# Modulation of a hybrid DeltaNet / RG-LRU layer in four parts of two channel tiles, with the loads, the parameter rows, two clearings and a weight split moved around it

## The chip, the cores and the metric

One core of one Trainium2 chip runs the whole program. The time is that of the device from the first to the last instruction, in microseconds (us); runs are given by their median. Engines are called TensorE (PE in the rows), VectorE (DVE), ScalarE (ACT), GpSimd (POOL) and SyncE (SP); nearly all loads of this stage are issued by SyncE.

## The reference

One layer of a diffusion trunk, for 128 context tokens and 1024 latent tokens of 1024 channels. What matters here is its head:

```python
shift, scale, gate = jnp.split(mod, 3, axis=-1)      # mod = silu(c) @ w_mod + b_mod, for c and for c_ctx
h = rmsnorm(x, p['norm_w']) * (1 + scale) + shift
proj = h @ p['w_in']                                 # 1024 x 6176, all in float32
```

Then come a gated DeltaNet of 8 heads, an RG-LRU, two output projections merged by gates, one more projection, a residual and a last RMSNorm. `w_mod` is 1024 x 3072; shift and scale are its first 2048 columns.

## The kernel before

All work is on tiles of 128 channels or 128 tokens: KT = 8 channel tiles `k`, NT = 9 token tiles `t` (one of context, eight latent), and NG = 3 groups `g` of three token tiles. Float32 products are made exact enough by splitting both sides in a high and a low float32r part: three matmuls for each tile. Each engine has its own hand-written list of instructions (`front_sync`, `front_gpsimd`, and the ScalarE, TensorE and VectorE functions of `front_stage`), and counters (`S["..."]`) order them. The lists are strictly sequential, so an instruction that waits holds all behind it on its engine.

The opening of the kernel, up to the first projection, goes so:

- **x.** A token tile of 512 KB is loaded (`x_load`), ScalarE squares and sums it (L736), GpSimd makes the reciprocal root (L518, L520), ScalarE scales the tile (`normalise`, L730), TensorE turns it in eight transposes (`turn_x`, L1019) and VectorE copies it from PSUM to `xt` in two halves (L1435).
- **Modulation.** `mod_load(n)` brings 512 KB of `w_mod`: one channel tile's rows, half of the shift and half of the scale columns, in runs of 2 KB. `modulate(n)` (L1010) multiplies it by silu(c) for both conditions, four matmuls of 256 columns in four column groups of the array; a float32 matmul stands in the trace as two records. Loads 0 to 7 make half 0 (gain and shift of channel tiles 0 to 3), loads 8 to 15 half 1 (tiles 4 to 7). `gain_and_shift` then copies a half to SBUF (L1450), has it turned (`turn_columns`, L1026) and adds the parameters (L1456 to L1459).
- **Parameters.** 18 small loads (`small_rows_in`, L397) are turned by three transposes (L1079) and copied to `par` (L1438) and scaled (L1440 to L1442). `wglo`, the low part of the gate weights, is made at L1445.
- **Rows.** For each channel tile VectorE writes gain times x plus shift into one of two buffers `hf` (L1464 context, L1468 latent), ScalarE rounds it to `hhi` (L748; by groups at L753 for tiles 0 and 4; L758 makes the latent rows of tiles 1 and 5), and VectorE subtracts for `hlo` (L1479, `low_rows`). TensorE runs `first_high(k)` (L1033, L1034, gate columns at L1037) and `first_low(k)` (L1043, L1048) of the first weight block; the second block starts with `project(1, 0)` (L134 to L136).
- **Filling.** `idle(n)` is n matmuls of the identity (L142) into a bank that nobody reads.
- **GpSimd** clears `w1` and `w2` (L553, L554) as soon as `modulate` has read the first four weight loads, which lie in them; then `low(0)` and `low(1)` (L528) make the low parts of weight blocks 0 and 1 from what ScalarE's `high(0)`, `high(1)` (L621) rounded.

In TensorE's list the modulations of half 0 stand between the turns of x, those of half 1 between channel tiles 0 to 3: three, three and two.

Of the kernel before, what the change touches and what calls it, by code (L numbers as in the profile page):

```python
# [125 lines left out]
def v3(ap):  # L126
    return ap.rearrange("p (j c) -> p j c", c=P)
# [35 lines left out]
def front_stage(nc, R, A, oa, rows, decay_rows, gate_rows, W):  # L163


    with ExitStack() as ctx:
# [24 lines left out]
        with nc.sbuf_tensor("wg_hl", [P, KT, 8 * H], F32R) as wghl:  # L191
# [25 lines left out]
        modrow = row2[:, 200:712].rearrange("p (a c) -> p a c", a=2)  # L217
# [48 lines left out]
            "wm2", "wm3", "x0", "x1", "x2", "x3", "wg_in", "h_fa", "rows_t", "par_done", "mod_k", "mod_row", "mod_t", "mod", "x_sq", "x_ms", "x_rstd", "x_n", "x_t",  # L266
# [75 lines left out]
        def mod_bank(half_):  # L342
            return bank[(2, 0)[half_]]

        def rows_done(k, g=NG - 1):
            return k + (NG - 1) * ((k + 3) // 4) + (g + 1 if k % 4 == 0 else 1)
# [10 lines left out]
        def front_sync(sp):  # L357
# [27 lines left out]
            def mod_load(n):  # L385
                half_, k = divmod(n, KT)
                if n >= NW:
                    sp.wait_ge(S[f"wm{n % NW}"], 16 * (n // NW))
                if n >= NOWN:
                    sp.wait_ge(S["mod_k"], KT)  # L390
                src = A["w_mod"][0, k * P:(k + 1) * P, 0:2 * D].rearrange("p (a c) -> p a c", a=2)
                sp.dma_start(wmod[n].rearrange("p (a c) -> p a c", a=2), src[:, :, half_ * 512:(half_ + 1) * 512]
                             ).then_inc(S[f"wm{n % NW}"], 16)
# [7 lines left out]
            x_load(0)  # L401
            x_load(1)
            mod_load(0)
            x_load(2)
            x_load(3)
            mod_load(1)
# [4 lines left out]
            mod_load(2)  # L411
            small_rows_in(1)
            x_load(6)
            x_load(7)
            mod_load(3)
            x_load(8)
            load(0)
            mod_load(4)
            sp.dma_start(wg, A["w_in"][0, :, 6 * D:6 * D + 4 * H].rearrange("(k p) n -> p k n", p=P)
                         ).then_inc(S["wg_in"], 16)  # L420
            for n in range(5, 2 * KT):
                mod_load(n)
# [87 lines left out]
        def front_gpsimd(pool):  # L510
# [11 lines left out]
            for padded in row:  # L522
                pool.memset(padded[:, 0:PAD_L], 0.0)
                pool.memset(padded[:, PAD_L + CTX:PAD_L + CTX + GAP], 0.0)
                pool.memset(padded[:, RAW - 1:RAW], 0.0).then_inc(S["clear"], 1)
# [25 lines left out]

            pool.wait_ge(S["mod_k"], 4)
# [63 lines left out]
        def front_scalar(act):  # L616
# [115 lines left out]
            for t in range(NT):  # L732
# [4 lines left out]
                if t:  # L737
                    normalise(t - 1)
# [6 lines left out]
            def high_rows(k):  # L745
                if k % 4:
# [221 lines left out]
        def front_tensor(pe):  # L968
# [29 lines left out]
            for half_ in range(2):  # L998
                for j in range(2):
                    keep_busy(pe, bank[half_][:, j * P:(j + 1) * P], ident, 4)  # L1000
# [5 lines left out]
            def modulate(n):  # L1006
                half_, k = divmod(n, KT)
                pe.wait_ge(S[f"wm{n % NW}"], 16 * (n // NW + 1))
                for i in range(Q):
                    mm = pe.matmul(bank[half_][mod_rows(i), 0:256], sc[:, :, k], wmod[n][:, i * 256:(i + 1) * 256],  # L1010
                                   start=(k == 0), stop=(k == KT - 1))
                mm.then_inc(S["mod_k"], 1)

            def turn_x(n):
                if n >= 2:
                    pe.wait_ge(S["x_e"], n - 1)
                pe.wait_ge(S["x_n"], n + 1)
# [5 lines left out]
            def turn_columns(half_):  # L1023
                pe.wait_ge(S["mod_row"], half_ + 1)
                for j in range(2):
                    mm = pe.transpose(mod_bank(half_)[:, j * P:(j + 1) * P], modrow[:, half_, j * P:(j + 1) * P], ident)  # L1026
                mm.then_inc(S["mod_t"], 1)

            def first_high(k):
                for g in range(NG):  # L1030
# [3 lines left out]
                    pe.matmul(bank[2 + g][:, 0:GW], wlo[:, 0, k, :], R.hhi[:, k, ts], start=False, stop=False)  # L1034
                for g in range(NG):
# [15 lines left out]

            modulate(0)
            idle(2)
            turn_x(0)
            turn_x(1)
            modulate(1)
            idle(2)
            turn_x(2)
            turn_x(3)
            idle(2)  # L1060
            modulate(2)
            idle(2)
            turn_x(4)
            turn_x(5)
            idle(2)
            modulate(3)
            idle(2)
            turn_x(6)
            turn_x(7)
            modulate(4)  # L1070
            idle(2)
            turn_x(8)
            modulate(5)
            idle(2)
            pe.wait_ge(S["rows_in"], 16 * len(sources))
            pe.wait_ge(S["x_e"], NT - 1)
            pe.wait_ge(S["c_done"], 1)
            for j in range(3):
                mm = pe.transpose(bank[4][:, j * P:(j + 1) * P], rows_in_[:, j, :], ident)  # L1079
            mm.then_inc(S["rows_t"], 1)  # L1080
            modulate(6)
            idle(2)
            modulate(7)
            idle(2)
# [3 lines left out]
            pe.wait_ge(S["wg_lo"], 1)  # L1088
            first_high(0)
            first_low(0)  # L1090
            modulate(8)
            modulate(9)
            modulate(10)
            first_high(1)
            first_low(1)
            modulate(11)
            modulate(12)
            modulate(13)
            first_high(2)
# [1342 lines left out]
```

## Time and profile before

| | |
|---|---|
| median of 3 runs | 1510.91 us (1510.03 to 1511.8) |
| the profiled execution, its own time | 1510.75 us |
| its span | 1509.0 us |
| busy share, TensorE / VectorE / ScalarE / GpSimd | 98% / 67% / 53% / 24% |
| first matmul of the first projection | 35.63 us after the start |
| first matmul of the second weight block | 65.29 us after the start |

A view of the timeline lists instructions in order: start, duration, engine, line, operation, output and inputs, shape, count; in brackets how long the engine was idle before it and what released it. Starts and durations are in us. "Windows" lists the busy time of each engine in a stretch. The stretch in which the changed instructions lie is the first 66 us.

### The profile page before, as it was taken

What the parts mean: (1) busy time and instruction counts of PE and PEld (TensorE: products, weight loads), DVE (VectorE), ACT (ScalarE), POOL (GpSimd) and SP (SyncE); (2) the same over time, 40 slices, a digit from 0 to 9 for tenths busy, and PEclk for the clock granted to TensorE, in tenths of its full rate; (3) what the DMA queues carried; (4) which work ended last, traced back from release to release, by engine and by line L of the source; (5) the groups of instructions that cost most, each with busy time, mean ns of one, the idle gap of its engine ahead of it and who ended that gap; (6) DMA issues with size and microseconds to landing.
All of it is one profiled execution on the core that took longest, in us unless ns stands there. A gap on an engine that the chain in (4) does not pass through costs nothing.

```text
span 1509.0 us, 27654 instructions
## 1 busy us (share of the span) xinstructions
PE 1479.6 (98%) x11204; PEld 1415.0 (94%) x11204; DVE 1010.0 (67%) x1776; ACT 796.1 (53%) x1639; POOL 359.9 (24%) x299
## 2 busy tenths in 40 slices
PE   7999999999999999999999999999999999999997
PEld 6799999999999999989799999999999999999886
DVE  4689898898989798898847736736737711434344
ACT  6484756758485756757356763663665510312111
POOL 3132223233232223223221212212212211232110
PEclk9999999999999999999999999999999999999999
DMA  9221112221312112321412121121221531443133
GB/s 340 82 67 56 58 45 78 62 78 33 108 33 73 54 45 78 104 79 60 126 43 67 52 80 58 55 77 58 62 71 62 182 134 43 164 145 103 43 102 121
DMA packets 118081, 127.44 MB, mean 84 GB/s; under 512 B 6489, under 2 KB 97474, under 8 KB 117954
## 3 DMA queue, kind: packets, MB, share of 16 engines
q1 hardware_dynamic: 117666, 125.34, 26.1%
q8 instruction: 89, 1.46, 0.4%
q14 instruction: 38, 0.31, 0.1%
q10 hardware_dynamic: 288, 0.33, 0.1%
HBM read 105.56 MB, written 20.09 MB: 83 GB/s over the span
## 4 chain that ended last, share of the span: by engine, by line
PE 90%; DVE 5%; ACT 2%; DMA 2%; issue 1%; SPq 0%; DVEq 0%; POOLq 0%; POOL 0%; ACTq 0%
PE mb L134 15%; PE mb L135 15%; PE mb L136 15%; PE db L134 9%; PE db L136 8%; PE db L135 8%; PE db L1327 3%; PE db L1299 2%; PE db L1343 2%; PE db L1316 2%; PE db L1337 2%; PE db L988 1%; PE db L1268 1%; DMA x_rows<-in_x_sample 1%; PE db L1186 1%
## 5 line engine op out<-in xcount | busy, mean ns | idle before, releaser
L134 PE MATMUL mb<-h_hi,w_hi 128*128 128x384 f32 x1080 | 363.3, 336 | 0.3 <-DVE h_lo L2292 0.3
L135 PE MATMUL mb<-h_lo,w_hi 128*128 128x384 f32 x1080 | 362.9, 336 | 0.0
L136 PE MATMUL mb<-h_hi,w_lo 128*128 128x384 f32 x1080 | 362.9, 336 | 0.0
L134 PE MATMUL db<-h_hi,w_hi 128*128 128x384 f32 x816 | 288.3, 353 | 2.2 <-ACT d_row L627 2.0
L136 PE MATMUL db<-h_hi,w_lo 128*128 128x384 f32 x816 | 274.7, 337 | 0.0
L135 PE MATMUL db<-h_lo,w_hi 128*128 128x384 f32 x816 | 274.7, 337 | 0.0
L1969 POOL TENSOR_TENSOR w_lo<-w,w_hi 128x1024 fp32r<-128x1024 f32 x47 | 129.0, 2746 | 462.6 <-ACT w_hi L1998 462.6
L134 PEld LDWEIGHTS mb<-h_hi,w_hi 128*128 128x128 f32 x1080 | 203.0, 188 | 1.0 <-DVE h_lo L2292 0.6
L136 PEld LDWEIGHTS mb<-h_hi,w_lo 128*128 128x128 f32 x1080 | 203.0, 188 | 0.0
L135 PEld LDWEIGHTS mb<-h_lo,w_hi 128*128 128x128 f32 x1080 | 203.0, 188 | 0.0
L134 PEld LDWEIGHTS db<-h_hi,w_hi 128*128 128x128 f32 x816 | 153.8, 189 | 6.3 <-issue 2.7
L135 PEld LDWEIGHTS db<-h_lo,w_hi 128*128 128x128 f32 x816 | 154.0, 189 | 0.0
L136 PEld LDWEIGHTS db<-h_hi,w_lo 128*128 128x128 f32 x816 | 153.5, 188 | 0.0
L1998 ACT ACTIVATE w_hi<-w 128x1024 fp32r<-128x1024 f32 x47 | 49.7, 1060 | 116.3 <-PE mb L136 74.0
L2252 DVE SCALAR_TENSOR_TENSOR l_tg<-l_tg,d_dt 128x1155 f32<-128x1155 f32 x16 | 36.6, 2328 | 95.3 <-ACT l_tg L2057 95.3
L1629 DVE TENSOR_TENSOR d_qg<-d_qg 128x31 f32<-128x31 f32 (+15 forms) x248 | 85.2, 343 | 8.5
L1627 DVE TENSOR_TENSOR d_qg<-d_qg 128x31 f32<-128x31 f32 (+15 forms) x248 | 84.5, 341 | 7.3
L929 ACT ACTIVATE d_vn<-db,d_nc 128x128 f32<-128x128 f32 x144 | 44.9, 363 | 78.2 <-DVE d_vk L1691 76.4
L528 POOL TENSOR_TENSOR w_lo<-w,w_hi 128x1024 fp32r<-128x1024 f32 x20 | 50.4, 2522 | 125.7 <-ACT w_hi L621 125.6
L590 POOL COPY d_w<-d_qg 32x288 f32<-32x288 f32 x32 | 22.7, 710 | 201.7 <-DVE d_qg L1639 200.8
L627 ACT ACTIVATE padded_rows<-db 128x128 f32<-128x128 f32 (+1 forms) x76 | 30.2, 429 | 68.3 <-PE db L136 67.9
L2313 DVE SCALAR_TENSOR_TENSOR mixed<-mixed,mb 128x384 f32<-128x384 f32 x24 | 13.0, 552 | 65.8 <-PE mb L136 65.8
(334 smaller groups left out, 2897.5 us busy)
## 6 DMA issues: line engine op xcount, KB each, us to landing
w<-in_w_in SPq DMA_DIRECT2D x48, 512.0 KB, 4.0
d_dt<-decay_rows SPq DMA_DIRECT2D x16, 576.0 KB, 6.6
d_qg<-decay_rows SPq DMA_DIRECT2D x16, 512.0 KB, 4.0
w<-in_w_gate SPq DMA_DIRECT2D x16, 512.0 KB, 4.4
branch_a<-d_kq SPq DMA_DIRECT2D x8, 576.0 KB, 3.2
branch_b<-l_z SPq DMA_DIRECT2D x8, 576.0 KB, 2.8
merge_gates_b<-l_gates SPq DMA_DIRECT2D x8, 576.0 KB, 5.5
m_in<-merge_gates_b SPq DMA_DIRECT2D x8, 576.0 KB
```

What stands on the lines that cost most here:

```text
L134: pe.matmul(out, hi, rhi, start=(k == 0), stop=False)
L135: pe.matmul(out, hi, rlo, start=False, stop=False)
L136: return pe.matmul(out, lo, rhi, start=False, stop=(last and stop))
L528: pool.tensor_tensor(wlo[:, j % 2], wst[:, :, :], whi[:, j % 2].bitcast(F32), ALU.subtract).then_inc(S["w_lo"], 1)
L627: ins = act.activation(dst[:, at:at + hi - lo], proj_bank(gi)[:, lo:hi], ACT.Copy)
L929: act.activation(vn[:, d, :], bank[3 + 2 * d][:, 0:P], ACT.Copy, scale=ncol[:, d, t:t + 1]).then_inc(S["vn"], 1)
L1327: pe.matmul(bank[3 + 2 * d][:, 0:P], vinv(d, t), vnu[:, d, :] if s else vt[:, t, :], start=True, stop=True).then_inc(S["p2"], 1)
L1627: link(dve.tensor_tensor(prod, amat[:, k * B + k + 1:(k + 1) * B].unsqueeze(2).broadcast_to([P, n, m]), xmat[:, k * B:k * B + m].unsqueeze ...
L1629: link(dve.tensor_tensor(low_rows, low_rows, prod, ALU.add))
L1969: pool.tensor_tensor(wlo_of(item), wst[:, slot(j)], whi_of(item).bitcast(F32), ALU.subtract).then_inc(S["w_lo"], 1)
L1998: act.activation(whi_of(item), wst[:, slot(j)], ACT.Copy).then_inc(S["w_hi"], 1)
L2252: dve.scalar_tensor_tensor(out=tg[:, 2 * d + 1, :], in0=tg[:, 2 * d + 1, :], scalar=1.0, in1=xc, op0=ALU.add, op1=ALU.mult).then_inc(S["p" ...
```

## The change

It splits the modulation in four parts, each of two channel tiles. A load `mod_load(n)` is now two DMAs of 256 KB with runs of 1 KB: the rows of two channel tiles, a quarter of the shift and of the scale columns. Loads 0 to 3 give part 0, which is all that channel tiles 0 and 1 need. `modulate(n)` is eight matmuls of 128 columns. SyncE's order becomes x 0 to 2, half of the small loads, x 3 and 4, `w_mod` 0, the other small loads, x 5 and 6, `w_mod` 1, x 7 and 8, weight block 0, and the rest; load 13 and those behind it still wait for eight modulations. Odd token tiles are normalised by VectorE. TensorE turns all x tiles with four filling matmuls between them, and does 4, 4 and 4 modulations before channel tiles 1, 2 and 3. The parameter rows follow the sixth x tile. VectorE copies the last half tile of x and makes `wglo` only after the rows of channel tile 0, and the gate columns of `first_high(0)` wait for both. GpSimd makes `low(0)` first and clears `w1` and `w2` once the low rows of channel tile 1 are there. ScalarE makes `high(1)` before channel tile 5 and no longer after 6.

```diff
@@ SyncE
+                for b in range(2):
+                    k = 2 * kk + b
+                    src = A["w_mod"][0, k * P:(k + 1) * P, 0:2 * D].rearrange("p (a c) -> p a c", a=2)
+                    sp.dma_start(wmod[n][:, b * 512:(b + 1) * 512].rearrange("p (a c) -> p a c", a=2),
+                                 src[:, :, part * 256:(part + 1) * 256]).then_inc(S[f"wm{n % NW}"], 16)
...
+            for t in range(3):
+                x_load(t)
             sp.wait_ge(S["rows_zero"], 1)
             small_rows_in(0)
+            x_load(3)
             x_load(4)
+            mod_load(0)
+            small_rows_in(1)
             x_load(5)
             x_load(6)
+            mod_load(1)
             x_load(7)
             x_load(8)
             load(0)
+            mod_load(2)
@@ GpSimd
+            low(0)
+            for padded in row:
...
             pool.wait_ge(S["mod_k"], 4)
+            pool.wait_ge(S["h_lo"], 2)
             pool.memset(w1[:, :, :], 0.0).then_inc(S["clear"], 1)
             pool.memset(w2[:, :, :], 0.0).then_inc(S["clear"], 1)
-            low(0)
@@ ScalarE
-                if t:
+                if t % 2:
                     normalise(t - 1)
...
             high_rows(4)
-            latent_rows(5)
-            act.wait_ge(S["h_fa"], 2)
+            high(1)
             high_rows(5)
             high_rows(6)
-            high(1)
             high_rows(7)
@@ TensorE
+                for b in range(2):
+                    for i in range(Q):
+                        mm = pe.matmul(mod_part(part, 0)[mod_rows(i), :], sc[:, :, 2 * kk + b],
+                                       wmod[n][:, b * 512 + i * P:b * 512 + (i + 1) * P],
+                                       start=(kk == 0 and b == 0), stop=(kk == KT // 2 - 1 and b == 1))
...
+            turn_x(0)
+            idle(4)
+            turn_x(1)
+            idle(4)
+            turn_x(2)
+            idle(4)
+            turn_x(3)
             modulate(0)
+            idle(4)
             turn_x(4)
+            idle(4)
             turn_x(5)
...
+            modulate(1)
+            idle(4)
+            turn_x(6)
+            idle(4)
+            turn_x(7)
+            idle(4)
+            turn_x(8)
+            modulate(2)
+            idle(4)
+            modulate(3)
+            idle(4)
             turn_columns(0)
             idle(5)
             low_done(pe, 0)
             first_high(0)
             first_low(0)
+            for k in range(1, 4):
+                for n in range(4 * k, 4 * k + 4):
+                    modulate(n)
+                first_high(k)
+                turn_columns(k)
+                first_low(k)
@@ VectorE
+            modulation_out(0)
+            gain_and_shift(0)
...
+            rows_by_groups(0)
+            context_rows(1).then_inc(S["h_f"], 1)
+            x_out(NT - 1, 1).then_inc(S["x_e"], 1)
+            dve.wait_ge(S["wg_hi"], 1)
+            dve.tensor_tensor(wglo, wg, wghi.bitcast(F32), ALU.subtract).then_inc(S["wg_lo"], 1)
+            low_rows(0)
+            modulation_out(1)
+            low_rows(1)
+            gain_and_shift(1)
+            whole_rows(2)
+            whole_rows(3)
+            modulation_out(2)
+            low_rows(2)
+            gain_and_shift(2)
+            dve.wait_ge(S["x_e"], NT + 1)
+            whole_rows(4)
+            low_rows(3)
+            modulation_out(3)
+            whole_rows(5)
+            gain_and_shift(3)
+            low_rows(4)
+            whole_rows(6)
+            low_rows(5)
+            whole_rows(7)
+            low_rows(6)
+            low_rows(7)
```

## Rows read from the trace of the kernel before

**Rows 1.** The page, busy time of each engine over the whole span.

```profile
PE 1479.6 (98%) x11204; PEld 1415.0 (94%) x11204; DVE 1010.0 (67%) x1776; ACT 796.1 (53%) x1639; POOL 359.9 (24%) x299
```

**Rows 2.** Windows: stretch, length, busy time of each engine, granted clock, DMA share, GB/s.

```profile
35.60:65.30 29.70, 26.95 (x187) 20.08 (x188) 19.73 (x27) 12.30 (x14) 2.40 (x1) 1.00 0.36 117
...
65.30:93.00 27.70, 27.70 (x171) 27.29 (x171) 20.63 (x43) 16.37 (x33) 6.90 (x3) 1.00 0.30 90
```

**Rows 3.** Timeline of TensorE in the opening.

```profile
3.11 6.47 PE L142 MATMUL db<-ident 128*128 128x128 f32 x32
...
16.90 1.06 PE L1019 MATMUL db<-ident,d_dt 128*128 128x128 f32 x8 [1.13 <-ACT d_dt L730]
...
17.80 0.61 PE L142 MATMUL db<-ident 128*128 128x128 f32 x4
...
30.49 0.62 PE L1010 MATMUL db<-w,silu_c 128*2 128x256 f32 x8
...
31.68 0.61 PE L1010 MATMUL db<-d_cb,silu_c 128*2 128x256 f32 x8
```

**Rows 4.** Timeline: the last x tile at ScalarE, and an x copy of VectorE.

```profile
23.59 1.06 ACT L736 ACTIVATE d_u<-x_rows 128x1024 f32<-128x1024 f32 x1 [0.23 <-DMA x_rows<-in_x_sample]
...
29.08 1.29 DVE L1435 COPY xt<-db 128x512 f32<-128x512 f32 x2 [0.77 <-PE db L1019]
```

**Rows 5.** Timeline of SyncE: the first nine small loads begin, and end before this.

```profile
4.47 0.52 SPq L397 DMA_DIRECT2D d_qg<-in_conv_a_w  x1
...
8.34 0.82 SPq L383 DMA_DIRECT2D x_rows<-in_x_sample  x2
```

**Rows 6.** DMA queues from 36 to 40 us, then from 60.3 to 64 us.

```profile
DMA packets 787, 1.51 MB, mean 378 GB/s; under 512 B 48, under 2 KB 48, under 8 KB 787
...
q1 hardware_dynamic: 1040, 0.52, 51.8%
```

**Rows 7.** Timeline of TensorE and VectorE around channel tiles 0 and 1.

```profile
34.20 0.35 DVE L1464 TENSOR_SCALAR d_u<-xt,gain,shift 128x128 f32<-128x128 f32 x1
...
35.63 0.42 PE L1033 MATMUL db<-h_hi,w_hi 128*128 128x384 f32 x1 [0.84 <-ACT h_hi L753]
...
36.34 1.36 DVE L1479 TENSOR_TENSOR h_lo<-d_u,h_hi 128x1152 fp32r<-128x1152 f32 x1 [0.44 <-ACT h_hi L753]
...
37.76 0.79 PE L1043 MATMUL db<-h_lo,w_hi 128*128 128x384 f32 x3 [0.25 <-DVE h_lo L1479]
...
38.00 0.81 DVE L1468 TENSOR_SCALAR d_u<-xt,gain,shift 128x1024 f32<-128x1024 f32 x1
...
39.00 0.62 PE L1010 MATMUL db<-d_q,silu_c 128*2 128x256 f32 x8
...
40.41 0.45 PE L1033 MATMUL db<-h_hi,w_hi 128*128 128x384 f32 x1
```

**Rows 8.** Groups of TensorE by line and form: busy us, mean ns of one.

```profile
L1191 PE MATMUL db<-ident,d_cb 128*32 128x1 f32 x576 | 6.2, 172 | 0.0
```

**Rows 9.** Timeline near the end of the loop over channel tiles.

```profile
57.81 2.40 POOL L528 TENSOR_TENSOR w_lo<-w,w_hi 128x1024 fp32r<-128x1024 f32 x1 [24.96 <-ACT w_hi L621]
57.87 4.83 DVE L1479 TENSOR_TENSOR h_lo<-d_u,h_hi 128x1152 fp32r<-128x1152 f32 x2
...
61.49 0.79 PE L1043 MATMUL db<-h_lo,w_hi 128*128 128x384 f32 x3 [1.46 <-DVE h_lo L1479]
```

**Rows 10.** Timeline: GpSimd and VectorE side by side, in three places.

```profile
25.90 2.02 POOL L553 MEMSET d_w<- 128x2304 f32 x1
...
29.83 2.37 POOL L528 TENSOR_TENSOR w_lo<-w,w_hi 128x1024 fp32r<-128x1024 f32 x1
...
31.19 1.04 DVE L1440 TENSOR_SCALAR par<-par 128x32 f32<-128x32 f32 x1
...
193.20 2.45 POOL L579 MEMSET d_u<- 32x576 f32 x4 [0.46 <-DVE w L1612]
194.47 0.19 DVE L1627 TENSOR_TENSOR d_qg<-d_qg 128x31 f32<-128x31 f32 x1
```

More of the change, by code:

```diff
@@ L340, in mod_rows, with mod_part @@
             return slice(i * B, i * B + 2)
-        def mod_bank(half_):
-            return bank[(2, 0)[half_]]
+        def mod_part(part, b):
+            return bank[b][:, part * P:(part + 1) * P]
         def rows_done(k, g=NG - 1):
-            return k + (NG - 1) * ((k + 3) // 4) + (g + 1 if k % 4 == 0 else 1)
+            return k + NG if k else g + 1
         def gate_parts(t):
@@ L521, in front_gpsimd @@
                                    ).then_inc(S["x_rstd"], 1)
[L522 to L525, printed above, removed]
             def low(j):
@@ L997, in front_tensor @@
             pe.transpose(bank[4][:, 0:2 * KT], crow, R.ident[0:2 * KT, 0:2 * KT]).then_inc(S["c_t"], 1)
-            for half_ in range(2):
-                for j in range(2):
-                    keep_busy(pe, bank[half_][:, j * P:(j + 1) * P], ident, 4)
+            for part in range(Q):
+                keep_busy(pe, mod_part(part, 0), ident, 4)
             pe.wait_ge(S["silu_c"], 1)
@@ L1006, in modulate @@
             def modulate(n):
[L1007 to L1011, printed above, removed]
+                part, kk = divmod(n, KT // 2)
+                pe.wait_ge(S[f"wm{n % NW}"], 32 * (n // NW + 1))
+                for b in range(2):
[3 more added lines that the diff above has]
+                                       start=(kk == 0 and b == 0), stop=(kk == KT // 2 - 1 and b == 1))
                 mm.then_inc(S["mod_k"], 1)
@@ L1016, in turn_x @@
                     pe.wait_ge(S["x_e"], n - 1)
-                pe.wait_ge(S["x_n"], n + 1)
+                if n % 2:
+                    pe.wait_ge(S["x_nd"], n // 2 + 1)
+                else:
+                    pe.wait_ge(S["x_n"], n // 2 + 1)
                 for k in range(KT):
@@ L1021, in turn_x, with turn_columns @@
                 mm.then_inc(S["x_t"], 1)
[L1023 to L1027, printed above, removed]
+            def turn_columns(part):
+                pe.wait_ge(S["mod_row"], part + 1)
+                pe.transpose(mod_part(part, 1), modrow[:, part, :], ident).then_inc(S["mod_t"], 1)
             def first_high(k):
@@ new lines, in front_vector, with modulation_out, gain_and_shift @@
+            x_out(NT - 1, 0).then_inc(S["x_e"], 1)
+            def modulation_out(part):
+                dve.wait_ge(S["mod_k"], (part + 1) * KT // 2)
+                dve.tensor_copy(modrow[:, part, :], mod_part(part, 0)).then_inc(S["mod_row"], 1)
+            def gain_and_shift(part):
+                k0, k1 = 2 * part, 2 * part + 2
+                per_k = lambda v: v[:, :, k0:k1].rearrange("p a i -> p i a")
+                par_k = lambda at: R.par[:, at + k0:at + k1].unsqueeze(2).broadcast_to([P, 2, 2])
+                turned_ = mod_part(part, 1).rearrange("p (i r) -> p i r", r=B)
+                dve.wait_ge(S["mod_t"], part + 1)
+                dve.tensor_tensor(per_k(gain), turned_[:, 2:4, 0:2], par_k(B_SCALE), ALU.add).then_inc(S["mod"], 1)
+                dve.tensor_tensor(per_k(shift), turned_[:, 0:2, 0:2], par_k(B_SHIFT), ALU.add).then_inc(S["mod"], 1)
+                dve.wait_ge(S["mod"], 2 * part + 2)
@@ L1484, in whole_rows @@
                 latent_rows(k, slice(CTX, TOK)).then_inc(S["h_f"], 1)
-            for half_ in range(2):
-                k = 4 * half_
-                gain_and_shift(half_)
-                if half_ == 0:
-                    dve.wait_ge(S["x_e"], NT)
-                    dve.wait_ge(S["x_sq"], NT)
-                rows_by_groups(k)
-                context_rows(k + 1).then_inc(S["h_f"], 1)
-                low_rows(k)
-                whole_rows(k + 2)
-                low_rows(k + 1)
-                whole_rows(k + 3)
-                low_rows(k + 2)
-                low_rows(k + 3)
+            modulation_out(0)
+            gain_and_shift(0)
+            dve.wait_ge(S["x_e"], NT)
+            dve.wait_ge(S["x_sq"], NT)
+            rows_by_groups(0)
[24 more added lines that the diff above has]
+            low_rows(7)
             conv(0, 0, (0, 1))
```

127 lines of the change are left out of this document (37 added, 90 removed).

## The prediction

> **What bounds the kernel now.** I read the page first: TensorE is busy for 98% of the span [rows 1]. From 65.3 to 93 us it is busy all the time, with 27.70 us of work in 27.70 us, at a granted clock of 1.00 [rows 2]. Nothing behind 65.3 us waits for a moment fixed from outside, so whatever moves the start of the second weight block moves the end by as much. The question is therefore how early `project(1, 0)` starts, which is 65.29 us now. In the stretch before it, from the first matmul at 35.6 us, TensorE is busy for 26.95 of 29.70 us [rows 2]. The timeline of the opening shows three limits in turn: TensorE's own list until the first half of the modulation is through, the hand-over of rows from VectorE over ScalarE until 39 us, then TensorE again with holes.
>
> **The change, part by part.** All times are in the profiled execution, 1510.75 us for a span of 1509.0, which is 0.16 us below the median of the runs shown, 1510.91.
>
> *The front, on TensorE's list.* The first filling ends at 3.11 + 6.47 = 9.6 us [rows 3] and stays. Then, up to the start of `modulate(3)`, the new list has nine turns, nine `idle(4)`, three modulations and three parameter transposes. A turn takes 17.80 − 16.90 = 0.90 us. A modulation with an `idle(2)` takes 31.68 − 30.49 = 1.19 us, some 0.55 of it the modulation; four records of the filling are then 0.45 (as half of a turn's eight), so `idle(4)` is 0.87 [rows 3]. That is 8.0 + 7.8 + 1.65 + 0.4 = 17.9 us: `modulate(3)` could start at 27.5. Two waits come on top. x tiles 4 and 6 are now scaled by ScalarE only behind the square of the next tile (`if t % 2`), which is 1.06 us [rows 4] after that one lands; I take 0.5 us for each. So `modulate(3)` starts at about 28.5, against `modulate(7)` at 31.68 now [rows 3].
>
> *Are the loads there?* The last x tile lands at 23.6 us now [rows 4], behind four weight loads; it will be behind two. Weight loads alone move at 378 GB/s, 1.39 us for 512 KB [rows 6]. Against that gain of 2.8 us stand two holes: the nine small loads hold SyncE for 8.34 − 4.47 = 3.87 us [rows 5], with three x tiles, 4.2 us of transfer, queued before the first nine, and three transfers before the second nine. I take 0.5 us for each. So the last tile lands at 21.8 and weight load 3, the fourteenth big transfer, at about 27.3, which is before TensorE comes for it. The price of runs of 1 KB is not in the trace. From below it is nothing (runs of 2 KB: 1.39 us a load); from above it is the rate of the lone `w_in` load, in runs of 512 B: 51.8% of 3.7 us for 512 KB, 1.92 us [rows 6]. That load includes its run-up, when the queue was not full, so I take the lower end.
>
> *From the last needed modulation to the first projection.* Now that is 35.63 − 31.68 = 3.95 us [rows 3, 7]. Two more `idle` matmuls (+0.45) meet `wglo` gone from VectorE's way (−0.35) and a copy of half the columns (−0.15): 3.9. The first matmul starts at 32.4, which is 3.2 us earlier.
>
> *Channel tile 0.* VectorE starts its rows 35.63 − 34.20 = 1.43 us before that, at 31.0 [rows 7]. It needs 1.7 us for five instructions of about 0.35 there [rows 7], then half an x copy, 0.65 [rows 4], and `wglo`, 0.45. So `low_rows(0)` starts 2.85 us after the rows and not 36.34 − 34.20 = 2.14, and the gate columns wait for `wglo` too. `first_low(0)` starts at 31.0 + 2.85 + 1.4 = 35.25, and the modulations follow 39.00 − 37.76 = 1.24 us later [rows 7], at 36.5. The lead is now 2.5 us.
>
> *Twelve modulations in the loop instead of eight.* Three of them take 40.41 − 39.00 = 1.41 us [rows 7], 0.43 each and 0.12 for the switch. With 128 columns each one has twice the matmuls of half the length, so it costs the same as long as the array time decides. The upper bound would be issue: the shortest matmuls here, one column wide, take 6.2/576 = 0.011 us each [rows 8], sixteen of them 0.17 us, so array time does decide. Now the way from 39.00 to 65.29 is 26.3 us. It holds the products of seven tiles, fifteen matmuls each; 21 of them take 65.29 − 61.49 = 3.80 us [rows 9], so a tile is 2.7 and seven are 19.0. Eight modulations with three switches are 3.8, the one turn of columns is 0.3. That is 23.1, so 3.2 us are holes: 1.46 ahead of tile 6's low part [rows 9], the rest mostly where tile 4 waits for the second `gain_and_shift` and its rows by groups. The new way has 19.0 + 5.5 for twelve modulations + 0.9 for three turns = 25.4 and whatever holes are left. I laid VectorE's list beside TensorE's (about 1.0 us for whole rows, 1.36 for low rows [rows 7]): the matmuls of tile 1 start at 38.4, those of tile 2 at 43.4, just behind ScalarE's rounding, those of tile 3 at 48.4. Nothing of note waits there.
>
> *The loads behind.* Load 13 now waits for the eighth modulation, at 38.5; it and the next three would land by about 45.5. The last is wanted at 47.9, which leaves 2.4 us of cover. If that is gone, tile 3 is late by the difference.
>
> *low(1).* Now `low(1)` of GpSimd meets VectorE at 57.81: two `low_rows` take 4.83 and not 2.7 us, and TensorE waits 1.46 us [rows 9]. In the new order it starts at about 49.6 and meets the last `gain_and_shift` and `low_rows(4)`; both read two tiles of SBUF. VectorE loses some 1.3 us and TensorE 0.8 of them. With 0.2 for small things, 1.0 us of holes is left. `high(1)` stands earlier on ScalarE, before tile 5; it holds that rounding by one such activation, about 1 us, and TensorE comes for it 3 us later.
>
> *The sum.* 36.5 + 25.4 + 1.0 = 62.9 for `project(1, 0)`, against 65.29: 2.4 us less. The time is 1510.75 − 2.4 = 1508.4 us.
>
> *The clearings.* This is the term that I can't read off. `w1` and `w2`, 2.02 us each [rows 10], now lie beside copies out of PSUM. In the new kernel they begin when `low_rows(1)` ends, near 40.3, and VectorE's `whole_rows(2)` and `whole_rows(3)` (one tile in, one out, in SBUF) fall in them. A GpSimd instruction that reads SBUF does hold such an instruction: L1440, 32 columns, started at 31.19 and took 1.04 us, until `low(0)` of GpSimd was over at 32.20; the one of 128 columns takes 0.35 [rows 7, 10]. A clearing does not hold an instruction with two inputs: 0.19 us for 31 columns inside four clearings [rows 10]. For one input beside a clearing there is no row; the bounds are nothing and all of it. I take nothing, by the row with a clearing in it, with doubt.
>
> The Trainium skill, "SBUF — State Buffer", section "SBUF: two separate sides", says that VectorE in a two-port mode and GpSimd exclude each other for a whole instruction, and that VectorE with two inputs is only excluded by a GpSimd instruction that reads SBUF. The row of L1440 and that of L1627 both agree with it; by that rule the clearings cost their full price, which is rival A.
>
> **The rivals.**
>
> *A. The clearings hold VectorE.* The context rows of tile 2 wait from 41.1 to 42.3, the second clearing then goes first and holds the latent rows until 44.6; they are 3.1 us late. TensorE has nothing to put there, and the slack at low(1) gives back nothing. `project(1, 0)` is at 65.9, 0.6 later than now: 1511.4. For it speaks L1440; against it L1627. If only one clearing is caught, 1.2 us are lost: 1509.6.
>
> *B. Nothing waits in the front either.* x tiles land in time for the ordered turns (−1.0), and `low(1)` falls between VectorE's instructions with two inputs (−0.8): 1506.6. For it speaks that ScalarE and VectorE now share the scaling; against it the order of ScalarE's list.
>
> *C. Runs of 1 KB move as slowly as those of 512 B,* on the other side. With a load at L us, the last lands at 27.3 + 4 (L − 1.39) + 12 L, and is wanted at 47.9: from L = 1.63 on each 0.1 us costs 1.6. At 1.92, with the holds in the front, about 4.5 us are lost: 1512.9. It turns slower than now at 1.78. Against it speaks the lone load's run-up [rows 6].
>
> The Trainium skill, "DMA: Bandwidth & Descriptors", section "Specifications", sets full rate from 512 B on; by that the sum stays.
>
> *D. TensorE's clock falls.* It is at the higher level, 2.4 GHz, in both stretches [rows 2]; the filling at the start runs at 6.47/32 = 0.20 us a record against 0.11 later [rows 3], the lower one. The new waits are shorter than 1.5 us, except in A, where one is 3.1. If it fell there, a tile's 2.7 us of products would take twice that: 1514.1.
>
> **How the numbers follow.** Forecast 0.38, A 0.32 (with one clearing 0.08 of it), B 0.15, C 0.08, D 0.02, something else 0.05. The own range of the likeliest is ±1.5 us, 1506.9 to 1509.9. The range to hold 8 in 10 takes in A and most of B: 1505.8 to 1512.2. A difference below 0.2%, 3.0 us, is what can't be told from none. Faster by more, under 1507.9: a third of the forecast, most of B, part of what I don't see: 0.28. Slower by more, over 1513.9: D, the worse ends of A and C, the rest: 0.08. Within: 0.64.
>
> **What would show it.** The first matmul of `first_high(0)` near 32.4 and `project(1, 0)` near 62.9; `modulate(3)` at 28.5; sixteen records of a modulation in 0.43 us. The rows of tile 2 at 0.35 and 0.81 us if the clearings don't hold them, over 1 and near 2 us if they do. The mean rate between 28 and 38 us above 360 GB/s. The prediction is wrong if TensorE waits for weight loads in the loop, or if the shift at 65 us isn't that of the end.

## The result, and the profile after

| | kernel before | changed kernel |
|---|---|---|
| median of the runs on the same chip, us | 1511.32 (16 runs, 1509.12 to 1514.22) | 1514.29 (16 runs, the fastest 1511.82) |
| ratio to the kernel before | 1 | 1.0017, 95% interval 1.0011 to 1.0024 |
| profiled execution: time, span, us | 1510.75, 1509.0 | 1514.12, 1512.3 |
| start of `first_high(0)`, us | 35.63 | 33.94 |
| start of `project(1, 0)`, us | 65.29 | 68.28 |

The slowest execution of the changed kernel, at 6793.9 us, is not in the ratio; the other 15 lie between 1511.82 and 1516.53 us. The changed kernel is 0.17% slower, 2.6 us of 1511.32. The forecast was 1508.4 us, with a range that ended at 1512.2. The difference is below the 0.2% that was set as "can't be told from none", but the interval doesn't reach 1.

The page of the changed kernel has this line for the engines, the one that answers to [rows 1]:

```profile
PE 1483.3 (98%) x11372; PEld 1423.9 (94%) x11372; DVE 1020.9 (68%) x1787; ACT 791.0 (52%) x1632; POOL 360.9 (24%) x299
```

TensorE is busy 3.7 us longer, in a span that is 3.3 us longer, so the loss must not be looked for in idle time alone. The next view to read is a table of windows: the way from the first matmul of `first_high(0)` to `project(1, 0)`, as long a stretch behind it as in [rows 2], and ten microseconds in the middle of that way. Its columns are those of [rows 2]. It is of the changed kernel.

```profile
33.90:68.30 34.40, 30.04 (x316) 24.73 (x317) 25.12 (x36) 10.88 (x11) 6.77 (x4) 0.95 0.49 154
68.30:96.00 27.70, 27.70 (x171) 27.29 (x171) 20.67 (x43) 16.38 (x33) 6.92 (x3) 1.00 0.31 91
...
45.00:55.00 10.00, 7.35 (x86) 6.09 (x87) 7.54 (x15) 4.34 (x4) 1.24 (x3) 0.83 0.47 137
```

Behind `project(1, 0)` TensorE is busy all the time, as before, so the change is over at 68.28 us. In front of it the granted clock is 0.95 and no longer 1.00 (0.83 from 45 to 55 us), and 4.4 us are idle. The start of that stretch is 1.7 us earlier than before, its end 3.0 us later.

The timeline of TensorE in the changed kernel shows where. First the front, then the loop.

```profile
11.50 1.06 PE L142 MATMUL db<-ident 128*128 128x128 f32 x8
14.41 1.06 PE L1021 MATMUL db<-ident,d_dt 128*128 128x128 f32 x8 [1.85 <-ACT d_dt L730]
...
19.25 1.06 PE L1021 MATMUL db<-ident,d_dt 128*128 128x128 f32 x8 [0.37 <-ACT d_dt L730]
...
30.19 0.62 PE L1008 MATMUL db<-d_w,silu_c 128*2 128x128 f32 x16
...
33.94 0.41 PE L1033 MATMUL db<-h_hi,w_hi 128*128 128x384 f32 x1 [0.82 <-ACT h_hi L753]
...
37.73 0.62 PE L1008 MATMUL db<-d_kn,silu_c 128*2 128x128 f32 x16
38.16 0.62 PE L1008 MATMUL db<-d_vt,silu_c 128*2 128x128 f32 x16
...
43.89 0.62 PE L1008 MATMUL db<-d_v,silu_c 128*2 128x128 f32 x16
47.65 0.44 PE L1033 MATMUL db<-h_hi,w_hi 128*128 128x384 f32 x1 [3.13 <-ACT h_hi L748]
...
48.73 0.52 PE L1034 MATMUL db<-h_hi,w_lo 128*128 128x384 f32 x1
49.05 1.16 PE L1040 MATMUL db<-h_hi,wg_hl 128*64 128x384 f32 x3
```

`modulate(3)`, the row at 30.19, starts 1.7 us later than the 28.5 forecast; ahead of it TensorE waits 1.85 us for x tile 2 (14.41) and 0.37 us for x tile 4 (19.25). The modulations in the loop follow each other by 0.43 us, sixteen records each, as forecast. Then, ahead of `first_high(2)`, TensorE is idle for 3.13 us, and 1.1 us behind that wait a matmul of the products takes 0.52 and not 0.34 us, three gate matmuls 1.16 and not 0.68: the clock is at the lower of its two levels, 1.2 and not 2.4 GHz.

What was late is in the timeline of VectorE and GpSimd at that place:

```profile
41.84 0.17 DVE L1459 TENSOR_TENSOR gain<-gain,par 128x4 f32<-128x4 f32 x1
42.04 3.82 DVE L1464 TENSOR_SCALAR d_u<-xt,gain,shift 128x128 f32<-128x128 f32 x1
42.30 4.09 DVE L1468 TENSOR_SCALAR d_u<-xt,gain,shift 128x1024 f32<-128x1024 f32 x1
46.32 0.33 DVE L1464 TENSOR_SCALAR d_u<-xt,gain,shift 128x128 f32<-128x128 f32 x1
46.57 0.80 DVE L1468 TENSOR_SCALAR d_u<-xt,gain,shift 128x1024 f32<-128x1024 f32 x1
...
41.40 2.02 POOL L554 MEMSET d_w<- 128x2304 f32 x1 [10.68 <-DVE h_lo L1479]
43.36 2.02 POOL L555 MEMSET d_w<- 128x2304 f32 x1
45.31 0.47 POOL L545 MEMSET w<- 128x448 f32 x1
```

The context rows of tile 2 (L1464) take 3.82 us and end at 45.86; those of tile 3, the same instruction, take 0.33. Three clearings of GpSimd lie over that time: `w1`, `w2` and, right behind them in its list, a short one (`clear_tail`, L545), which ends at 45.78. The rows end 0.08 us behind it. So all three went ahead of an instruction that was issued while the first one ran. The third was not in the prediction: in the kernel before it waits for the eighth modulation, which here is through before the clearings start.

The front is explained by ScalarE's squares of x tiles and by SyncE's issues. In the changed kernel ScalarE shows

```profile
12.08 1.06 ACT L736 ACTIVATE d_u<-x_rows 128x1024 f32<-128x1024 f32 x1 [2.50 <-DMA x_rows<-in_x_sample]
16.92 1.06 ACT L736 ACTIVATE d_u<-x_rows 128x1024 f32<-128x1024 f32 x1 [1.61 <-DMA x_rows<-in_x_sample]
21.68 1.06 ACT L736 ACTIVATE d_u<-x_rows 128x1024 f32<-128x1024 f32 x1 [1.53 <-DMA x_rows<-in_x_sample]
```

where x tiles 3, 5 and 7 are waited for, and SyncE's queue shows the small loads that hold them back, nine from 2.86 us and nine from 8.02 us on:

```profile
2.86 0.43 SPq L399 DMA_DIRECT2D d_qg<-in_conv_a_w  x1
...
8.02 0.98 SPq L399 DMA_DIRECT2D d_qg<-in_lru_lambda_fwd  x1
...
11.76 0.89 SPq L383 DMA_DIRECT2D x_rows<-in_x_sample  x2
```

From 8 to 20 us the loads moved 309 GB/s at a share of 0.93, so the queues ran empty at times.

### The profile page after: what moved, and what is told of

The parts are those of the page before. It is cut to its first block, busy times and chain, and to the rows that moved or that the text cites. A ratio compares the mean times of both kernels' runs of the same rounds, so it can differ in the third digit from the quotient of the medians.

```text
span 1512.3 us, 28012 instructions
## 1 busy us (share of the span) xinstructions
PE 1483.3 (98%) x11372; PEld 1423.9 (94%) x11372; DVE 1020.9 (68%) x1787; ACT 791.0 (52%) x1632; POOL 360.9 (24%) x299
## 3 DMA queue, kind: packets, MB, share of 16 engines
q8 instruction: 90, 1.47, 0.4%
## 4 chain that ended last, share of the span: by engine, by line
PE 91%; DVE 4%; ACT 2%; issue 1%; DMA 1%; SPq 1%; POOL 0%; DVEq 0%; POOLq 0%; ACTq 0%
PE mb L134 15%; PE mb L136 15%; PE mb L135 15%; PE db L134 9%; PE db L136 8%; PE db L135 8%; PE db L1315 3%; PE db L1287 2%; PE db L1331 2%; PE db L1304 2%; PE db L1325 2%; PE db L986 1%; PE db L1256 1%; PE db L1174 1%; PE db L1141 1%; DVE d_qg L1645 1%
```

## The experiments

The table gives what decides in each: the start of `first_high(0)`, how far behind it `project(1, 0)` starts, and the ratio of the runs to the kernel before on the same chip. The difference of the two starts takes the front out; from one execution of a kernel to the next the front alone moves by up to 1.1 us.

| kernel | `first_high(0)` | from there to `project(1, 0)` | `project(1, 0)` | ratio, 95% interval |
|---|---|---|---|---|
| before | 35.63 | 29.66 | 65.29 | 1 |
| changed | 33.94 | 34.34 | 68.28 | 1.0017 (1.0011 to 1.0024) |
| both clearings early | 34.32 | 30.37 | 64.69 | 0.9999 (0.9990 to 1.0009) |
| one clearing early | 33.64 | 30.37 | 64.01 | 0.9996 (0.9987 to 1.0004) |
| small loads later | 31.06 | 34.21 | 65.27 | 1.0001 (0.9992 to 1.0010) |
| both edits | 31.56 | 29.53 | 61.09 | 0.9977 (0.9968 to 0.9986) |
| both, `low(1)` last | 31.31 | 28.75 | 60.06 | 0.9968 (0.9957 to 0.9978) |
| the same, less filling | 30.95 | 28.75 | 59.70 | 0.9968 (0.9957 to 0.9980) |
| before, `low(1)` last | 35.24 | 27.89 | 63.13 | 0.9989 (0.9981 to 0.9998) |
| before, runs of 1 KB | 38.73 | 29.65 | 68.38 | 1.0012 (1.0003 to 1.0021) |
| changed, 28 fillings | 34.11 | 35.76 | 69.87 | 1.0043 (1.0031 to 1.0055) |
| changed, 12 fillings | 33.72 | 32.26 | 65.98 | 1.0011 (1.0002 to 1.0019) |
| changed, second profile | 34.48 | 32.71 | 67.19 | one run |
| changed, third profile | 33.40 | 34.17 | 67.57 | one run |

**Both clearings early.** The theory: the clearings hold VectorE, and the wait lets the clock fall. One line of GpSimd's list:

```diff
             pool.wait_ge(S["mod_k"], 4)
-            pool.wait_ge(S["h_lo"], 2)
+            pool.wait_ge(S["x_e"], NT + 1)
             pool.memset(w1[:, :, :], 0.0).then_inc(S["clear"], 1)
```

> The changed kernel with one wait replaced: the two clearings of w1 and w2 on GpSimd start when the last half of the x copy is through (near 34.8 us) and no longer when low_rows(1) is through (41.4 us). From 34.8 to 38.9 us VectorE has only wglo, low_rows(0) and a copy out of PSUM. Theory (the clearings hold VectorE's one-input instructions in SBUF, and the wait that comes of it lets TensorE's clock fall): the rows of tile 2 take 0.34 and 0.81 us instead of 3.82 and 4.09, first_high(2) starts near 44.4 us instead of 47.65, the clock stays at its higher level, project(1, 0) starts near 63.5 us instead of 68.28; the time is 4.8 us below the changed kernel and 2.2 us below the kernel before. Rival (the loss has another cause: loads, rounding on ScalarE, more modulations): project(1, 0) stays at 68 us. Second rival (only the hold counts, the clock's fall has another cause): 65.1 us.

The timeline of VectorE and GpSimd of this run:

```profile
35.11 0.41 DVE L1494 TENSOR_TENSOR wg_hl<-d_kq,wg_hl 128x256 fp32r<-128x256 f32 x1
35.31 2.02 POOL L554 MEMSET d_w<- 128x2304 f32 x1 [4.17 <-DVE xt L1429]
35.44 1.35 DVE L1479 TENSOR_TENSOR h_lo<-d_u,h_hi 128x1152 fp32r<-128x1152 f32 x1
...
42.41 0.35 DVE L1464 TENSOR_SCALAR d_u<-xt,gain,shift 128x128 f32<-128x128 f32 x1
42.67 0.81 DVE L1468 TENSOR_SCALAR d_u<-xt,gain,shift 128x1024 f32<-128x1024 f32 x1
...
51.84 2.39 POOL L523 TENSOR_TENSOR w_lo<-w,w_hi 128x1024 fp32r<-128x1024 f32 x1 [11.23 <-ACT w_hi L621]
51.96 2.29 DVE L1459 TENSOR_TENSOR gain<-gain,par 128x4 f32<-128x4 f32 x1
```

The rows of tile 2 take 0.35 and 0.81 us, and `first_high(2)`, at 44.82, has no wait ahead of it. `first_high(2)` is 10.50 us behind `first_high(0)` and not 13.71, so the hold by the three clearings costs 3.2 us (the short one, at 40.12 us here, meets no rows either). A clearing that lies over `low_rows(0)`, with two inputs, leaves it at 1.35 us. `low(1)`, which reads SBUF, does hold an instruction with two inputs: the last one of `gain_and_shift(3)`, on 4 columns, takes 2.29 us, and TensorE then waits 1.42 us for the low rows of tile 4. That wait, 0.7 us longer than in the changed kernel, and a front 0.4 us later are why this run came out at 64.69 and not 63.5. The time was forecast 2.2 us below the kernel before and is equal to it within 0.1%; the difference of 0.6 us at `project(1, 0)` agrees with that.

**One clearing early.**

```diff
-            pool.wait_ge(S["h_lo"], 2)
+            pool.wait_ge(S["x_e"], NT + 1)
             pool.memset(w1[:, :, :], 0.0).then_inc(S["clear"], 1)
+            pool.wait_ge(S["h_lo"], 2)
             pool.memset(w2[:, :, :], 0.0).then_inc(S["clear"], 1)
```

> As the run with both clearings early, but only w1 is cleared early; w2 still starts when low_rows(1) is through, at 41.3 us, and ends at 43.3. Theory: the context rows of tile 2 are held until 43.4 and end at 43.7, the latent rows end at 44.5, first_high(2) starts near 45.7 us, a wait of about 1.3 us on TensorE; too short for the clock to fall, so project(1, 0) is at 64.8 us, 1.3 us behind the run with both early. If the clock falls after this wait too: 66.4. Rival (the clearings cost nothing): no difference between the two runs.

VectorE and GpSimd in this run:

```profile
41.73 1.40 DVE L1465 TENSOR_SCALAR d_u<-xt,gain,shift 128x128 f32<-128x128 f32 x1
...
43.58 0.57 DVE L1465 TENSOR_SCALAR d_u<-xt,gain,shift 128x128 f32<-128x128 f32 x1
...
41.03 2.02 POOL L556 MEMSET d_w<- 128x2304 f32 x1 [4.37 <-DVE h_lo L1480]
42.98 1.09 POOL L545 MEMSET w<- 128x448 f32 x1
```

The clearing of `w2` ran from 41.03 to 43.05 us, the context rows of tile 2 from 41.73 to 43.13. Behind that clearing VectorE went first: the short clearing took 1.09 us here and not 0.47, and then held the context rows of tile 3, which took 0.57. TensorE waited 0.71 us ahead of `first_high(2)` and kept its clock. The 1.3 us behind the run with both early were not seen: both are 30.37 us long, because here the wait for `low(1)` was 0.67 and not 1.42 us. The hold of this run was given back there.

**Small loads later.**

```diff
-            for t in range(3):
+            for t in range(4):
                 x_load(t)
             sp.wait_ge(S["rows_zero"], 1)
             small_rows_in(0)
-            x_load(3)
             x_load(4)
-            mod_load(0)
-            small_rows_in(1)
             x_load(5)
+            mod_load(0)
             x_load(6)
-            mod_load(1)
             x_load(7)
+            small_rows_in(1)
+            mod_load(1)
             x_load(8)
```

> The changed kernel with the small loads later on SyncE: four x tiles ahead of the first nine, and x tiles 4 to 7 and the first weight load ahead of the second nine. Theory (small loads hold SyncE and so the x tiles, which hold the front): x tiles 3, 5 and 7 are squared without the waits of 2.50, 1.61 and 1.53 us, modulate(3) starts at 28.7 us instead of 30.19, first_high(0) at 32.5 instead of 33.94; the clearings cost what they did, so that project(1, 0) is at 66.8 and the time 1.4 us below the changed kernel. Rival (TensorE's own list and ScalarE's order set the front): modulate(3) stays at 30.2 and the time the same.

`modulate(3)` is at 27.31 us and `first_high(0)` at 31.06, 2.9 us earlier than in the changed kernel and 1.4 earlier than expected: TensorE has no wait left in the front. From 8 to 20 us the loads move 348 GB/s at a share of 1.05, against 309 at 0.93. The loop costs what it did: 3.13 us of wait, a clock of 0.85 from 45 to 55 us, 34.21 us to `project(1, 0)`.

**Both edits at once.**

> Both edits at once: the clearings start when the x copy is through, and the small loads stand later on SyncE. Alone they took 3.97 us off the way from first_high(0) to project(1, 0) (34.34 to 30.37) and 2.9 us off the start of first_high(0) (33.94 to 31.06). Theory (two separate causes): first_high(0) near 31.0, project(1, 0) near 61.4 if the loads of the third part are there, up to 62.4 if tile 3 waits for the last one; the time is 3 to 4 us below the kernel before, ratio near 0.9977. Rival (the two overlap, for the loads now set the loop): project(1, 0) at 64 or later, and the time is that of the kernel before.

`project(1, 0)` is at 61.09 us, and no modulation of the loop waits for a transfer (one in the front waits 0.15 us). The two causes add up to within 0.3 us of the 61.4 expected; the front came 0.5 us later than with the loads moved alone, and the wait at `low(1)` was 0.60 and not 1.42 us. The ratio is the one expected.

**Filling matmuls in the wait,** to price the clock alone.

```diff
                     modulate(n)
+                if k == 2:
+                    pe.wait_ge(S["mod"], 4)
+                    keep_busy(pe, mod_part(3, 1), ident, 28)
                 first_high(k)
```

> The changed kernel, clearings where they are, with 28 filling matmuls of 128 columns (about 3.0 us) in TensorE's list behind the modulations of part 2 and ahead of first_high(2); nothing else. Theory: first_high(2) starts at 47.65 us as before, for the rows are as late; but the engine has worked until about 46.7, the granted clock stays at 1.00, the products of tile 2 take 2.7 us and not about 4.2, and project(1, 0) is at 66.7 us, 1.6 us earlier. Rival (the products are slow for another reason than the wait): 68.3 us, the same.

> The run with filling matmuls again, with 12 instead of 28 (one takes 0.22 us and leaves two records, so 28 took 6.3 us and ran past the wait): 2.7 us of filling, which end near 47.2 us, before the rounded rows of tile 2 are there. Theory (the clock falls because TensorE waits 3.13 us): first_high(2) at 47.65 us as in the changed kernel, granted clock 1.00 from 45 to 55 us, project(1, 0) at 66.7 us, 1.6 us earlier, and the time 1.6 us below the changed kernel. Rival: 68.3 us and the same time.

28 of them were too many: they took 6.3 us, two records each, and `first_high(2)` started only at 50.87. But with the clock at 1.00 it was 19.00 us from there to `project(1, 0)`, against 68.28 − 47.65 = 20.63 us in the changed kernel. With 12, the filling ended as `first_high(2)` began at 46.91, and it was 19.07 us from there. So the lower clock costs 1.6 us. Whether filling keeps the clock up these two runs don't show, for it also stayed up once without (below). The run with 12 can't show what it was made for, since the hold was different in it. Its VectorE and GpSimd:

```profile
41.80 1.46 DVE L1467 TENSOR_SCALAR d_u<-xt,gain,shift 128x128 f32<-128x128 f32 x1
42.06 1.73 DVE L1471 TENSOR_SCALAR d_u<-xt,gain,shift 128x1024 f32<-128x1024 f32 x1
43.72 2.12 DVE L1467 TENSOR_SCALAR d_u<-xt,gain,shift 128x128 f32<-128x128 f32 x1
...
41.16 2.02 POOL L554 MEMSET d_w<- 128x2304 f32 x1 [10.66 <-DVE h_lo L1482]
43.12 2.63 POOL L555 MEMSET d_w<- 128x2304 f32 x1
45.70 1.09 POOL L545 MEMSET w<- 128x448 f32 x1
```

Here VectorE got in between the two clearings: tile 2's context rows end at 43.26, and the second clearing holds those of tile 3. Behind it VectorE goes first again, and the short clearing takes 1.09 us.

**The changed kernel again, twice.**

> The changed kernel once more, unaltered, for a second look at its clearings. In the run with 28 filling matmuls both clearings went ahead of the context rows of tile 2 (3.82 us), in the run with 12 only the first (1.46 us, and the rows of tile 3 then waited 2.12 us). If VectorE's place in between is a matter of the moment, one of the looks shows the one and another the other; if it is fixed for this program, both show 3.82 us. With both held: first_high(2) 13.7 us behind first_high(0), project(1, 0) 34.3 behind it; with one: near 11.9 and 30.9.

> A third look at the changed kernel, for the same question: 3.82 us at the context rows of tile 2 and project(1, 0) 34.3 us behind first_high(0) if both clearings go first, about 1.4 us there and 30.9 if VectorE gets in between them.

Both show the long hold, 3.83 and 3.82 us, behind all three clearings, and 3.13 us of wait on TensorE; with the first profile, that is three of three. (The expectation counts two clearings.) But the clock differs. The windows from 45 to 55 us, second profile and then third:

```profile
45.00:55.00 10.00, 6.87 (x96) 5.86 (x93) 8.42 (x16) 4.84 (x5) 2.06 (x3) 1.00 0.49 147
```

```profile
45.00:55.00 10.00, 7.90 (x89) 6.63 (x90) 7.38 (x15) 4.46 (x5) 1.02 (x2) 0.83 0.40 109
```

In the second profile the clock stayed at 1.00 after the same 3.13 us, and `project(1, 0)` is 67.19 − 48.17 = 19.02 us behind `first_high(2)`, as in the runs with filling; in the third it is 67.57 − 47.10 = 20.47, 1.45 us more. The clock fell in three of four executions with that wait, the run with the small loads later among them.

**`low(1)` last.** On top of both edits:

```diff
-            high(1)
             high_rows(5)
             high_rows(6)
             high_rows(7)
+            high(1)
```

> Both edits, and high(1) of ScalarE behind high_rows(7) instead of ahead of high_rows(5), so that low(1) of GpSimd runs from about 58.5 us on, when VectorE is through with its rows or nearly so. Theory (low(1) holds VectorE wherever both read SBUF; in the run with early clearings it held the last instruction of gain_and_shift(3) for 2.29 us and TensorE then waited 1.42 us): TensorE has no wait of note from tile 4 on, but project(1, 0) waits for low(1) some 0.5 us; in all 0.9 us earlier than the run with both edits, near 60.5 us. Rival (the wait moves to the end in full, for low(1) is then last): the same as the run with both edits, or later.

`low(1)` runs from 56.18 to 58.81 us, behind VectorE's rows but for the last 0.36 us of `low_rows(7)`, and is through before TensorE comes for it at 60.06. The window over the way from `first_high(0)`:

```profile
31.30:60.00 28.70, 28.22 (x315) 23.67 (x316) 19.72 (x36) 10.84 (x11) 7.09 (x4) 1.00 0.57 177
```

Of 28.70 us 28.22 are busy. This is the fastest order found, at 0.9968, 4.8 us below the kernel before. What `low(1)` last adds to the two edits is 0.8 us of the way in the profiles; the intervals of the two ratios overlap, so the times don't show it.

**The same move in the kernel before.**

> The kernel before with one line moved: high(1) of ScalarE behind high_rows(7), as in the run with low(1) last. It asks what of that run's time is the new order's own. Theory (low(1) beside low_rows(5) and low_rows(6) costs TensorE the 1.46 us wait in the old order too): the wait is gone, project(1, 0) waits little or nothing for low(1), and is at 64.0 to 64.4 us instead of 65.29; the time is 0.9 to 1.3 us below the kernel before. The new order with all three edits stays 3 to 4 us ahead of it. Rival (low(1) is then the last and is waited for in full): 65.3 us or later and the same time.

`project(1, 0)` is 27.89 us behind `first_high(0)` and not 29.66, and the 1.46 us wait is gone; the ratio is 0.9989, 1.7 us. So some 1.7 of the 4.8 us could be had in the old order (by the interval, 0.3 to 2.9). The rest, about 3.1, is the new order's, once its two faults are mended.

**Less filling** at three places of the front, `idle(2)` for `idle(4)`, six matmuls fewer (the expectation says four places; the kernel has three).

> The run with all three edits, with two filling matmuls instead of four at four places of the front (behind the turns of x tiles 6 and 7 and behind modulations 2 and 1 of the last three). Theory (with the loads in time TensorE's own list sets the front: it was busy all the time from 13 to 30 us): eight matmuls fewer or less of 0.22 us each, so first_high(0) and project(1, 0) are up to 1.7 us earlier, less what the last x tile or VectorE holds; I expect 0.8 us. Rival (x tile 8, squared at 20.8 us, or the weight loads of the loop set the time): no difference, and a wait on a transfer shows in the front or at the modulations of tile 3.

`first_high(0)` is 0.36 us earlier and the ratio unchanged. ScalarE waits 1.59 us for x tile 8, TensorE 0.34 us for that tile, which it turns at 25.01 us, no earlier than with the full filling (24.96): the loads are the limit there again. The 0.8 us were not had.

**Runs of 1 KB in the kernel before.**

```diff
-                sp.dma_start(wmod[n]..., src[:, :, half_ * 512:(half_ + 1) * 512])
+                for b in range(2):
+                    sp.dma_start(wmod[n]...[:, :, b * 256:(b + 1) * 256],
+                                 src[:, :, half_ * 512 + b * 256:half_ * 512 + (b + 1) * 256])
```

> The kernel before, with each of its sixteen weight loads issued as two of 256 columns of either side, so in runs of 1 KB instead of 2 KB; nothing else. It prices rival C. Theory (runs of 1 KB cost little): 28 to 40 us moves 355 to 360 GB/s instead of 381, so 1.47 us for 512 KB instead of 1.39; modulate(7) and first_high(0) start 0 to 0.5 us later, project(1, 0) near 65.5, and the time is within 0.5 us of the kernel before. Rival C (1.6 us or more for 512 KB): modulate(7) starts 1.7 us later and the time is 1.5 us or more above.

Here my expectation was wrong: `first_high(0)` is 3.1 us later, and the ratio is 1.0012, 1.8 us. From 28 to 40 us it moved 317 GB/s and not 381 (378 in the part of it that [rows 6] shows), but at a share of 0.97, so the queues were also not full: the run doubles SyncE's issues as well. In the front TensorE waited 2.87 us for a scaled tile, and its clock was 0.86 from 16 to 28 us. So this run shows that more and shorter transfers in the load-bound front of the old order cost up to 3 us (3.1 in the profile, 1.8 by the median); it doesn't part run length from issues and clock. For the changed kernel the price is in its own trace: from 28 to 38 us, with a share above 1, it moved 357 GB/s in runs of 1 KB, 1.47 us for 512 KB. In its two later profiles it was 340 and 339 GB/s, 1.54 us. The sign set for this, above 360, was missed.

## Why the prediction was wrong

**The step that failed** is "The clearings. ... I take nothing, by the row with a clearing in it, with doubt". That row, L1627, has two inputs, and those are indeed not held by a clearing (1.35 us for `low_rows(0)` under one). In the changed kernel an instruction with one input and its output in SBUF is held for as long as the clearing lasts, and in three of three profiles for the next two as well: 3.82 us for what takes 0.33. Rival A had the mechanism and the place, and it should have been the main case instead of being given 0.32: the nearer row to an unknown with one input was L1440, also with one input, and not L1627. That its size was right, rows 3.1 us late forecast and 3.2 measured by the run with the clearings moved, is partly luck: A let VectorE in between the two clearings, which didn't happen, and had nothing for the third, of 0.47 us. By itself the hold leaves the time in the stated range (1508.4 + 3.2 = 1511.6); it takes the front and the clock to leave it.

The Trainium skill, "SBUF — State Buffer", section "SBUF: two separate sides", gives the shared port pair to whichever instruction starts first, for the whole of it, and frees two-input instructions of VectorE from GpSimd instructions that don't read SBUF. The traces agree in all four combinations: 1.40 us for one input under one clearing and 3.82 under three in a row, 1.35 us (none lost) for two inputs under a clearing, 2.29 us for two inputs under `low(1)`, and 2.90 us for one input under it, the last in these rows of the changed kernel:

```profile
54.55 2.38 POOL L523 TENSOR_TENSOR w_lo<-w,w_hi 128x1024 fp32r<-128x1024 f32 x1 [8.76 <-ACT w_hi L621]
54.59 2.90 DVE L1468 TENSOR_SCALAR d_u<-xt,gain,shift 128x1024 f32<-128x1024 f32 x1
```

In the prediction this rule stood beside the term, and the term was set against it.

**The clock.** D followed from A, was given 0.02, and its 2.7 us are 1.6 measured: the clock falls 1.1 us behind the wait and is back as tile 2's products end, so tile 2 takes 4.48 us (47.65 to 52.13) against 2.93 in the second profile, and not twice its time. D's time, 1514.1, is close to the measured 1514.29, but only because its sum lacks the front's 1.5 us and has too much for the clock.

**The front.** "I take 0.5 us for each" was too small, and one wait was missing. The prediction names x tiles 4 and 6 as scaled behind the square of the next tile. Tile 2 is too, and it cost TensorE 1.85 us, tile 4 0.37 and tile 6 nothing of note: 2.2 us and not 1.0. Behind that are the small loads: x tiles 3, 5 and 7 were waited for 2.50, 1.61 and 1.53 us by ScalarE. The hold of SyncE was covered on paper by three x tiles of transfer ahead of it, but tile 3 was issued at 6.17 and was there near 12.0 us, 5.8 us later; the three tiles ahead of it were through long before. TensorE's own work up to `modulate(3)` was mis-sized too, 19.1 us and not 17.9, since an `idle(4)` behind a modulation takes about 1.1 us and not 0.87; against that the first turn starts at 8.86 and not at 9.6. These sum to the 1.7 us by which `modulate(3)` is late: 1.2 + 1.2 − 0.7. The way from `modulate(3)` to `first_high(0)`, 3.9 us forecast, is 3.75.

**The loop without the clearings** came out as forecast, 62.9 − 32.4 = 30.5 us against 30.37 with the clearings early, but two errors cancel in it. The wait at `low(1)` was put at 0.8 us and was 1.42 there; without it the loop is 28.95 us, where 29.7 were forecast. Right in it are the twelve modulations at 0.43 us and that no weight load is waited for (those of tile 3 were issued from 39.78 us on). The wait at `low(1)` was 0.71 us in the changed kernel and 0.54 to 1.42 in the others with `low(1)` at that place, by which instruction it met.

**The sum of the miss:** 62.9 + 1.5 (front) + 3.2 (clearings) + 1.6 (clock) − 0.8 (the rest of the loop) − 0.1 (`low(1)`, 0.71 for 0.8) = 68.3, measured 68.28. The shift at 65 us, +3.0, is that of the span, +3.3, within the spread; the runs have +2.6.

**Rival C** is out: 1.47 to 1.54 us for 512 KB is below the 1.63 from which it would have cost anything. **Rival B** has its first half in the run with the small loads later (`modulate(3)` at 27.31, where B had 27.5; the two errors in TensorE's own time nearly cancel there).

**Open:** what decides whether VectorE or GpSimd goes first where both wait at the end of a clearing (GpSimd in all three profiles of the changed kernel, with the small loads later and with 28 filling matmuls; VectorE with 12 and with one clearing early), and why the clock fell in three of four executions behind the same wait.

## What to carry to other kernels

When work of GpSimd is moved, lay it against the kind of instruction that VectorE runs at the new place: in these traces those with one input in SBUF were held by the clearings and by `low`, those with two inputs only by `low`, which reads SBUF. Look also at what follows the moved work in GpSimd's list, for it comes along, as the third clearing did. Here the good place was behind the last copy out of PSUM, six microseconds earlier (35.31 for 41.40) and one line away. And when small loads stand between large ones, count from issue to landing, not the transfer time alone: what was issued ahead must last until the next large one lands.

## What the runs showed of the hardware

- A clearing of 128 x 2304 on GpSimd (2.02 us) stops an instruction with one input on VectorE until it is over: 1.40 us for what takes 0.34, with one clearing early. Three in a row (2.02, 2.02 and 0.47 us) stopped it for all three: 3.82 us, in five profiles of kernels in that order.
- Under `low(1)` an instruction of 4 columns took 2.29 us for 0.17, one of 1024 columns 2.90 for 0.81: both lost 2.1 us.
- It works the other way too: where VectorE got in between, GpSimd's second clearing took 2.63 and not 2.02 us, and the short one 1.09 and not 0.47.
- TensorE's clock fell to its lower level behind a wait of 3.13 us in three executions (two of the changed kernel, one with the small loads later) and not in a fourth, of the changed kernel. It also fell behind the 2.87 us in the front of the run with runs of 1 KB, and stayed at 1.00 behind 2.11 us in the front of the run with both clearings early.
